# Rows of the cumulative gates: one turn, a scratch in HBM and eight DMAs to all partitions in place of 32 turns on TensorE

## The reference

```python
def gated_delta_rule_chunked(q, k, v, g, beta):
    ...
    g = jnp.cumsum(g, axis=-1)
    decay = jnp.exp(jnp.where(incl, g[..., :, None] - g[..., None, :], -jnp.inf))
    k_beta = k * beta[..., None]
    m = jnp.where(strict, jnp.einsum('bhncd,bhnsd->bhncs', k_beta, k) * decay, 0.0)
    t_inv = lax.linalg.triangular_solve(eye + m, ...)
    ...
    a_intra = jnp.where(incl, jnp.einsum('bhncd,bhnsd->bhncs', q, k) * decay, 0.0)
```

## Time and profile before

| what | value |
|---|---|
| median of 3 runs (lowest to highest) | 936.87 us (934.18 to 937.03) |
| the profiled execution: its own time | 935.59 us |
| its span in the trace | 933.8 us |
| TensorE busy (matmul) | 908.8 us, 97% |
| VectorE, ScalarE, GpSimd busy | 491.3, 455.0, 466.7 us |
| chain of work that ended last, by engine | PE 77%, DVE 11%, ACT 5%, POOL 4% |
| mean granted TensorE clock | 0.997 |

### The profile page before, as it was taken

The page is one execution under the profiler, slowest core; times in us unless marked ns, Lnnn a source line. Parts: engine busy times, 40 slices in busy tenths (PEclk is TensorE's granted clock), DMA queues, the critical chain, the costliest instruction groups (busy, mean ns, idle before and its releaser), DMA issues.

```text
span 933.8 us, 11971 instructions
## 1 busy us (share of the span) xinstructions
PE 908.8 (97%) x4752; PEld 765.2 (82%) x4752; DVE 491.3 (53%) x814; ACT 455.0 (49%) x806; POOL 466.7 (50%) x264
## 2 busy tenths in 40 slices
PE   8999999899999999999999899999999999999997
PEld 6988778799998788788787788888888888888885
DVE  5679826888857533433654535333333334654434
ACT  6665597676534434547556236343333434423223
POOL 4454443987476424446768424444444444354440
PEclk9999999999999999999999999999999999999999
DMA  9522300000022624332231214223332222233202
GB/s 344 184 92 89 113 23 1 1 2 1 1 91 70 239 67 135 100 104 68 69 91 46 89 47 137 91 90 106 99 111 91 90 91 91 88 120 108 90 23 91
DMA packets 25303, 83.63 MB, mean 90 GB/s; under 512 B 3008, under 2 KB 3264, under 8 KB 25120
## 3 DMA queue, kind: packets, MB, share of 16 engines
q1 hardware_dynamic: 24240, 81.49, 26.2%
q10 hardware_dynamic: 1008, 1.38, 0.4%
HBM read 78.66 MB, written 2.10 MB: 86 GB/s over the span
## 4 chain that ended last, share of the span: by engine, by line
PE 77%; DVE 11%; ACT 5%; POOL 4%; issue 1%; DMA 1%; SPq 0%; DVEq 0%; POOLq 0%; ACTq 0%
PE bank L2148 75%; PE bank L2156 3%; DVE qk L1645 2%; DVE vc L1645 1%; ACT L1285 1%; POOL nh L1185 1%; POOL wl L1136 1%; DVE vg L1639 1%; DVE r L1639 1%; DVE dt L1639 1%; DMA xt<-in_xt 1%; DVE bank L1639 0%; POOL mb L1148 0%; ACT vc L1285 0%; DVE swr L1639 0%
## 5 line engine op out<-in xcount | busy, mean ns | idle before, releaser
L1136 POOL TENSOR_TENSOR wl<-raw,wh 128x1024 fp32r<-128x1024 f32 (+1 forms) x129 | 310.1, 2409 | 372.5 <-ACT wh L1285 372.5
L2148 PE MATMUL bank<-xh,wh 128*128 128x512 f32 (+1 forms) x536 | 206.9, 386 | 1.1 <-DVE xl L1639 1.1
L2148 PE MATMUL bank<-xl,wh 128*128 128x512 f32 (+1 forms) x536 | 205.2, 383 | 0.0
L2148 PE MATMUL bank<-xh,wl 128*128 128x512 f32 (+1 forms) x528 | 202.2, 383 | 0.0
L1285 ACT ACTIVATE wh<-raw 128x1024 fp32r<-128x1024 f32 (+2 forms) x132 | 135.9, 1036 | 126.5 <-PE bank L2148 120.6
L2148 PE MATMUL bank<-wh,xh 128*128 128x512 f32 (+1 forms) x352 | 140.1, 398 | 2.5 <-DVE xl L1639 1.6
L2148 PE MATMUL bank<-wh,xl 128*128 128x512 f32 (+1 forms) x352 | 134.4, 382 | 0.0
L2148 PE MATMUL bank<-wl,xh 128*128 128x512 f32 (+1 forms) x352 | 134.0, 381 | 0.0
L2148 PEld LDWEIGHTS bank<-xh,wh 128*128 128x128 f32 x536 | 100.8, 188 | 20.8 <-issue 1.5
L2148 PEld LDWEIGHTS bank<-xl,wh 128*128 128x128 f32 x536 | 100.8, 188 | 19.2
L2148 PEld LDWEIGHTS bank<-xh,wl 128*128 128x128 f32 x528 | 99.2, 188 | 19.4
(11 more groups left out here) (270 smaller groups left out, 1436.6 us busy)
## 6 DMA issues: line engine op xcount, KB each, us to landing
raw<-in_wflat SPq DMA_DIRECT2D x126, 512.0 KB, 3.5
xt<-in_xt SPq DMA_DIRECT2D x8, 256.0 KB, 4.5
h<-in_x SPq DMA_DIRECT2D x4, 512.0 KB, 7.1
h<-in_x SPq DMA_DIRECT2D x1, 2048.0 KB, 7.5
gain<-in_pr SPq DMA_DIRECT2D x3, 512.0 KB, 3.6
consts<-in_cf SPq DMA_DIRECT2D x1, 1088.0 KB, 9.7
raw<-in_wflat SPq DMA_DIRECT2D x4, 272.0 KB, 10.7
kh<-kh SPq DMA_DIRECT2D x8, 128.0 KB, 2.3
```

What stands on the lines that cost most here:

```text
L1136: e.tensor_tensor(WL[u % NS][:, 0:n], RAW[u % NS][:, 0:n], WH[u % NS][:, 0:n].bitcast(F32), ALU.subtract).then_inc(w_lo.up(u), 1)
L2148: return e.matmul(o, l, r_, start=start, stop=stop, skip_group_check=part)
```

## The change

`gates()` gets a third step, behind the convolution's j = 6. There TensorE turns all of `GC` at once (128 x 32 to 32 x 128), and VectorE copies the result from PSUM to a new tile `GR`. SyncE stores `GR` (16 KB) in a scratch tensor in HBM, `gate_rows`. ScalarE then starts eight DMAs (`decay_rows`), one for each chunk and direction, each of which reads four rows of 128 and writes them to all 128 partitions of an `EE` tile (256 KB). Two of them stand ahead of the z pieces and six behind its piece 5. The 32 turns and VectorE's eight additions go. ScalarE's absolute value becomes four instructions of 128 columns, each with the `NGC` column of its head as bias; the exponential stays as it was.

```diff
@@ gates()
+        G.take("gate_turn", (gate_v, "rows"))
+        do("gate_turn")
+        yield
@@ invert(cb)
-            take(("gc", d), (inv_v, ("ee0", cb, d)))
             do("inv_decay", cb, d)
@@ the convolution's loop over j
+        if j == 6:
+            step(g2)
+        if j == 7:
+            do("gate_store")
@@ around the z pieces
+    do("decay_rows", 0)
     for n in tok_pieces(U_Z, "z"):
+        if n == 5:
+            for cb in (3, 1, 2):
+                do("decay_rows", cb)
@@ sync_engine
+        def gate_store():
+            on.wait_ge(*gate_v.at("rows"))
+            e.dma_start(gate_rows, GR[:]).then_inc(s_rows, 16)
@@ scalar_engine
+        def decay_rows(cb):
+            on.wait_ge(s_rows, 16)
+            on.wait_ge(*{0: norm_a.at(("ss", 0, 3)), 3: rope_p.at(4)}.get(cb, dense.at((U_Z, 3))))
+            for d in range(2):
+                r = (d * 4 + cb) * 4
+                e.dma_start(WORK[cb]["EE"][d][:].rearrange("p (h n) -> p h n", h=4), gate_rows[r:r + 4, :].partition_broadcast(128)).then_inc(s_row[cb], 16)
+
         def inv_decay(cb, d):
             ee = WORK[cb]["EE"][d][:]
-            on.wait_ge(*inv_v.at(("ee0", cb, d)))
-            act(ee, ee, ACT.Abs, inv_a.up(("ee1", cb, d)))
+            on.wait_ge(s_row[cb], 32)
+            on.wait_ge(*gate_v.at("ngc"))
+            for h in range(4):
+                act(hs(ee, h), hs(ee, h), ACT.Abs, inv_a.up(("ee1", cb, d) if h == 3 else ("ee1", cb, d, h)), bias=NGC[:, d, cb, h:h + 1])
@@ vector_engine
+        def gate_turn():
+            b, _ = BANK["gate_turn"]
+            on.wait_ge(*gate_p.at("turn"))
+            e.tensor_copy(GR[:], psum[b][0:32, 0:128]).then_inc(gate_v.up("rows"), 1)
-        def inv_decay(cb, d):
...
-            tt(h3(WORK[cb]["EE"][d][:]), h3(psum[b][:, :]), b4r(NGC[:, d, cb, :]), ALU.add, inv_v.up(("ee0", cb, d)))
@@ tensor_engine
+        def gate_turn():
+            p = bank("gate_turn")
+            on.wait_ge(*gate_v.at("gc"))
+            tr(p[0:32, 0:128], GC[:].rearrange("p d c h -> p (d c h)")).then_inc(gate_p.up("turn"), 1)
-        def inv_decay(cb, d):
...
-            for h in range(4):
-                t = tr(hs(p, h), GC[:, d, cb, h:h + 1].broadcast_to([128, 128]))
```

More of the change, by code:

```diff
@@ L323, in program @@
     SWO = zb("swo", [128, 512], F32, 122)
+    GR = zb("gr", [32, 128], F32, 129)
     OT = zb("ot", [128, 512], F32, 129)
@@ L368, in program @@
     s_w_first = sem("s_w_first")
+    s_rows, s_row = sem("s_rows"), [sem(f"s_row{c}") for c in range(4)]
     s_xagain, s_b2 = sem("s_xagain"), sem("s_b2")
@@ L1036, in swa_keys @@
         return k0, (k1 - k0 + 1) * 128
+    gate_rows = nc.dram_tensor("gate_rows", (32, 128), F32, kind="Internal").ap()
     unit0 = wflat[0:128 * 1024].rearrange("(p n) -> p n", p=128)
@@ L1119, in end @@
             on.wait_ge(s_out[1], 64)
-        return dict(begin=begin, load=load, x_again=x_again, b2_load=b2_load, twice=twice, gain=gain, finish=finish, end=end)
+        return dict(begin=begin, load=load, gate_store=gate_store, x_again=x_again, b2_load=b2_load, twice=twice, gain=gain, finish=finish, end=end)
     def pool_engine(e):
@@ L1626, in scalar_engine @@
         return dict(begin=begin, x_split=x_split, rms_row=rms_row, prep=prep, prep_half=prep_half, stat=stat, split=split, conv_copy=conv_copy, silu=silu, square=square, qsum=qsum, qexp=qexp, to_tok=to_tok,
-                    gate1=gate1, gate2=gate2, rope_sq=rope_sq, rope_root=rope_root, rope_keys=rope_keys, rope_t=rope_t, tok=tok, tok_end=tok_end, inv_decay=inv_decay, inv_mr=inv_mr,
+                    gate1=gate1, gate2=gate2, rope_sq=rope_sq, rope_root=rope_root, rope_keys=rope_keys, rope_t=rope_t, tok=tok, tok_end=tok_end, decay_rows=decay_rows, inv_decay=inv_decay, inv_mr=inv_mr,
                     inv_x=inv_x, inv_d=inv_d, swa_e=swa_e, swa_t=swa_t, scan_v=scan_vn, scan_av=scan_av, scan_oq=scan_oq,
@@ L2133, in finish @@
                 stt(OUT[:, tb, c], H[:, tb, c], rr, GAIN[:, c], ALU.mult, ALU.mult, fin_v.up(("out", tb, n)))
-        return dict(begin=begin, x_split=x_split, conv_rms=conv_rms, scale=scale, split=split, masks=masks, conv=conv, qexp=qexp, gate_dt=gate_dt, gate_beta=gate_beta, gate2=gate2, rope_tables=rope_tables, rope_sq=rope_sq,
-                    rope_root=rope_root, rope=rope, rope_keys=rope_keys, rope_k=rope_k, rope_t=rope_t, inv_decay=inv_decay, inv_mb=inv_mb, inv_q=inv_q, inv_m=inv_m,
+        return dict(begin=begin, x_split=x_split, conv_rms=conv_rms, scale=scale, split=split, masks=masks, conv=conv, qexp=qexp, gate_dt=gate_dt, gate_beta=gate_beta, gate2=gate2, gate_turn=gate_turn, rope_tables=rope_tables, rope_sq=rope_sq,
+                    rope_root=rope_root, rope=rope, rope_keys=rope_keys, rope_k=rope_k, rope_t=rope_t, inv_mb=inv_mb, inv_q=inv_q, inv_m=inv_m,
                     inv_mt=inv_mt, inv_x=inv_x, inv_d=inv_d, inv_x7=inv_x7, inv_t=inv_t, swa_s=swa_s, swa_o=swa_o,
@@ L2323, in tensor_engine @@
         sub = lambda t_, h: t_[:, h * 128:(h + 1) * 128]
-        def inv_decay(cb, d):
-            p = bank(("inv", cb, "gc", d))
-            on.wait_ge(*gate_v.at("beg"))
-            on.wait_ge(*gate_a.at("egl"))
-            for h in range(4):
-                t = tr(hs(p, h), GC[:, d, cb, h:h + 1].broadcast_to([128, 128]))
-            t.then_inc(inv_p.up(("gc", cb, d)), 1)
         def inv_k(cb):
@@ L2582, in tensor_engine @@
         return dict(begin=begin, split=split, ch=ch, narrow=narrow, ch_part=ch_part, tok=tok, tok_first=tok_first, tok_a=tok_a, tok_b=tok_b, last0=last0, last=last, pair=pair, qsum=qsum, to_tok=to_tok,
-                    gate2=gate2, rope_t=rope_t, inv_decay=inv_decay, inv_k=inv_k, inv_q=inv_q, inv_mt=inv_mt, inv_x=inv_x, rms_row=rms_row,
+                    gate2=gate2, gate_turn=gate_turn, rope_t=rope_t, inv_k=inv_k, inv_q=inv_q, inv_mt=inv_mt, inv_x=inv_x, rms_row=rms_row,
                     inv_d=inv_d, inv_x7=inv_x7, inv_t=inv_t, swa_s=swa_s, swa_t=swa_t, swa_o=swa_o, scan_ks=scan_ks, scan_qs=scan_qs, scan_v=scan_vn,
```

## The result

| | median us (lowest to highest, runs) | profiled execution | span | mean granted clock |
|---|---|---|---|---|
| before | 937.12 (933.75 to 939.49, 20) | 935.59 | 933.8 | 0.997 |
| after | 938.95 (936.45 to 941.84, 20) | 938.31 | 936.3 | 0.993 |

The ratio is 1.0022, 95% interval [1.0013, 1.0031]: about 2 us slower. The interval does not contain 1, so the slowdown is clear of the noise, but it is smaller than the 0.3% that the prediction called slower. The prediction was 941.0 us with a range of 936.5 to 944.0. A span in this document is that of the one execution that was profiled. Executions of one kernel differ by some us (the 20 spans of after run from 934.4 to 939.8), so a difference of a few tenths between two spans tells nothing without the rows behind it.

A forecast was written before the change was run, and what follows sets the result against it. TensorE, busy for 908.8 of 933.8 us, was taken to set the time. The terms, 3.25 + 1.7 + 0.9 - 0.8 = +5.05 us, on a base of 935.9 gave 941.0 us, range 936.5 to 944.0.

The forecast's parts named there:

- the rival in which the clock holds: TensorE's clock does not fall behind the gap at 114: +3.35 us, 939.3 us; chance 0.24.
- Term 1: At `qsum` 0: the moved bank makes it wait for VectorE's last convolution, +3.25 us (bounds 3.1 and 3.4).
- term 2: Behind TensorE's new gap at 114: the granted clock falls, +1.7 us (bounds 0 and 3.4).
- Term 3: Chunk 0's two DMA starts on ScalarE delay the turned queries and TensorE's second turn of v, +0.9 us (bounds 0 and 1.8).
- Term 4: From the decays to chunk 2's turn: TensorE comes forward only 0.8 us, limited by GpSimd; -0.8 instead of -4.0.
- The removed turns become a wait for GpSimd: At chunk 3's turn: TensorE arrives some 3 us early and waits over 2 us for GpSimd.
- The second fall of the clock: At TensorE's wait for GpSimd at chunk 3's turn: the clock falls again, making the clock's cost up to 3.4 us.
- the early decays pay in full: At the decays: DMA starts and narrow absolute values cost ScalarE next to nothing; -3.65 us, 932.3 us; chance 0.06.

The follow-up runs named there:

- e2: The kernel before with only the ring of banks advanced by one behind the convolution's j = 6; 942.06 us, ratio 1.0068.
- e3: The changed kernel with five unread sums on TensorE ahead of `qsum` 0, in the bank of `qsum` 1; 937.85 us, ratio 1.0013.
- e6: e1 with all eight row DMAs started by SyncE; 933.67 us, ratio 0.9969.
- e5: e1 with one absolute value of 512 columns in place of four of 128, leaving three heads' decays wrong; 933.41 us, ratio 0.9961.
- e4: e1 with the 32 turns kept on TensorE, their results unread; 935.50 us, ratio 0.9988.
- e1: The changed kernel, but the added turn of `GC` reuses bank 6 and the ring of banks is not advanced; 934.40 us, ratio 0.9983.
- e7: e1 with the addition and the absolute value on VectorE, ScalarE only the exponential; 944.63 us, ratio 1.0078.
- e9: e1 with VectorE's addition back, on rows that came by DMA, and one 512-column absolute value on ScalarE; 939.29 us, ratio 1.0029.

## Why the prediction came out as it did

The direction was right and the time 2 us too high, in part by luck. The base of 935.9 us was 1.2 below the median of before (937.12), which hid part of the miss: the forecast was a slowdown of 5.05 us, the medians show 1.8 and the spans 2.5. The outcome "slower by over 0.3%", with a chance of 0.75, didn't come. The time lies closest to the rival in which the clock holds (939.3), and yet the clock fell. By its own terms, in spans:

- **Term 1 and term 2, +3.25 and +1.7: right.** The first turn of the gate z, at 144.62 in after and at 139.53 before, is 5.09 us late against 4.95. e2 shows the same 5.09 from the ring alone. The split was a little off: e3 puts 1.5 on the clock, which leaves 3.6 for the wait, above its bound of 3.4. VectorE ended the convolution 0.41 us late where 0.15 had been put, and the two errors nearly cancel.
- **Term 3, +0.9: wrong, measured 0.** TensorE's second turn of v, which waits for the queries' copies behind the two starts, is 5.11 us late, and the turn at 144.62, which doesn't, 5.09. The price of 0.45 us a start was right (0.33 to 0.48), but a start lies beside the running activation. That was the lower bound given, and e6 fits it: 0.2 us of span for all eight.
- **Term 4, -0.8: too small by 1.7; this is the step that failed.** It charged 2.7 us for six starts ahead of the decays. They took 2.77, but beside the four copies of the keys, so that only 0.45 shows: the price was right and the overlap was missing. ScalarE came to the decays at 157.36: 154.22 + 5.10 less 1.96, not 0.3 later. The dearer absolute values took 0.65 of that back (0.45 were predicted, and e5 measures 0.57), so GpSimd's first mask came at 161.39, 1.3 us early by the count of terms 1 and 2, not 0.6 late. The rest of the working holds with that number in it: TensorE's last turn of chunk 2 had 1.37 us of play; 1.37 + 1.3 = 2.7 could come forward, and 5.10 - 2.59 = 2.5 did. The bound of 0 for a start had been named at term 3 and not carried into term 4, where it was worth three times as much.
- **The removed turns become a wait for GpSimd: right,** 2.39 us at chunk 3 against "over 2", and in e4 3.5 us of turns cost nothing up to chunk 2's turn.
- **The second fall of the clock,** named as the upper bound of term 2, did come, behind that wait of 2.39 us. It cost little: TensorE is busy for 4.64 us from 175 to 180, where before it waited for ScalarE in the same work. How much of it reaches the end wasn't tried in after; e4, without that fall, is 0.34 us ahead of e1 at chunk 2's last turn.

With terms 1 and 2 at +5.1, term 3 at 0 and term 4 at -2.5 the sum is +2.6; the spans differ by 2.5. The rival "the early decays pay in full" described the right mechanism in part, since starts were next to free. It asked for a mask 3.5 us early, and got 1.3.

e1's span gains 1.6 us, though by its turn of chunk 2 at 185.11 it was 2.3 ahead. The other 0.7 goes at 195. VectorE, GpSimd and TensorE of e1, and VectorE's same instruction before:

```profile
193.38 1.55 DVE L1666 TENSOR_TENSOR es<-rparams,mx 128x8 f32<-128x8 f32 x1
...
189.86 5.05 POOL L1193 TENSOR_TENSOR mp<-ds,consts 128x512 f32<-128x512 f32 x4
...
195.59 0.67 PE L2172 MATMUL bank<-xf,xf 128*128 128x192 f32 x4 [0.55 <-DVE xf L1666]
```

```profile
195.70 0.35 DVE L1639 TENSOR_TENSOR es<-rparams,mx 128x8 f32<-128x8 f32 x1
```

A tiny addition of 8 columns, with both operands in SBUF, ends when GpSimd's run ends (194.91), 1.2 us longer than before; the next step of VectorE is late by that, TensorE waits 0.55 us for it, and its lead over before falls from 2.3 to 1.6 us. In e4, e5 and e6 the same addition took 0.40, 0.82 and 0.64 us. It is a matter of where it falls beside GpSimd's instructions, and it is the stretch of e7 and e9 once more. What stays open is how the cost divides in e9, what after's second fall of the clock costs, and why e4's clock fell at 295 and e6's did not at 170.

## What to carry to other kernels

When a step is added to a list whose buffers are dealt out in turn, look first at what every later step now waits for: here that was worth 5 us, more than all that the change meant to move, and was undone by reusing a bank that was already free. Work taken from the busiest engine is worth nothing where the next thing it does waits for another engine; count what that engine gains. A span of one execution that agrees with a theory isn't enough: e5 came out at its number while each of its signs failed, so compare the two kernels row by row until the difference appears. And when a bound is named for one occurrence of a cost, put it at every other occurrence before summing.

## What the runs showed of the hardware

- A DMA start on ScalarE's queue takes 0.33 to 0.48 us and overlaps with activations that are under way: of the six starts from 154.49 to 157.26 in after 0.45 us shows, behind the last copy.
- The clock fell to 0.5 for some 3.4 us behind a wait of TensorE of 2.38 us in e1 and 2.39 in after, and not behind the same 2.39 us in e6. Before, waits of 1.64 and 1.77 us were followed by no fall, and two of 1.8 us together at 295 by a fall in e4 alone. No length of a wait separates these.
- VectorE's steps with no bank among their operands take 0.69 us alone and up to 1.79 beside GpSimd (128x512); those with a bank stay at 0.69. A step of 8 columns went from 0.35 to 1.55 us.
